# A hybrid decoder step on one core: the attention projections multiply raw x, and the token scale is applied where tiles leave PSUM

## The reference

```python
def rmsnorm(x, g):
    y = xf * lax.rsqrt(jnp.mean(xf * xf, axis=-1, keepdims=True) + EPS)
    return (y * g.astype(jnp.float32)).astype(x.dtype)
...
    h = rmsnorm(x, g)                       # norm_kv
    k, v, fl = jnp.split(h @ w_kv, [D_ATT, 2 * D_ATT], axis=-1)
    logf = jax.nn.log_sigmoid(fl.astype(jnp.float32) + b_f.astype(jnp.float32))
...
    h = rmsnorm(x, g)                       # norm_b
    q, z = jnp.split(h @ w_in, 2, axis=-1)
    o = attend(q.reshape(Bg, T, N_HEADS, HEAD_DIM))
    y = o.reshape(Bg, T, D_ATT) * jax.nn.silu(z)
    return x + y @ w_out
```

## Time and profile before

| | |
|---|---|
| median of 3 runs | 1842.98 us (1842.9 to 1845.61) |
| the profiled execution | 1851.57 us, its span 1850.0 us |
| mean granted TensorE clock | 0.959 of full speed |
| PE busy | 1728.3 us, 93% of the span |
| DVE busy | 848.5 us, 46% |
| ACT busy | 668.2 us, 36% |
| POOL busy | 314.9 us, 17% |

### The profile page before, as it was taken

One profiled execution on the slowest core, in us unless ns is written; L12 is line 12 of the kernel. 1 busy time (PEld: TensorE's weight loads), 2 busy tenths in 40 slices (PEclk: granted clock), 3 DMA queues, 4 the chain that ended last, 5 costly groups with the idle time before them and its releaser, 6 DMA issues.

```text
span 1850.0 us, 31228 instructions
## 1 busy us (share of the span) xinstructions
PE 1728.3 (93%) x10991; PEld 1568.5 (85%) x10991; DVE 848.5 (46%) x1349; ACT 668.2 (36%) x1096; POOL 314.9 (17%) x339
## 2 busy tenths in 40 slices
PE   6999999999999988999999999999866999998997
PEld 5999999999989988888888888888744666668997
DVE  4433333333253366555565556555545333323333
ACT  5211111112043235565655556565534222213322
POOL 4111111100000011222222122222112222210110
PEclk8999999999999989999999999999968999995998
DMA  4111111111201133111101021111225888882002
GB/s 146 36 47 47 47 47 47 47 39 42 75 29 43 29 120 97 37 47 36 58 24 58 24 69 51 43 47 36 86 87 193 306 318 295 330 265 68 29 28 97
DMA packets 173147, 165.08 MB, mean 89 GB/s; under 512 B 19756, under 2 KB 149948, under 8 KB 172966
## 3 DMA queue, kind: packets, MB, share of 16 engines
q1 hardware_dynamic: 162342, 129.51, 22.5%
q0 software_dynamic: 10752, 34.89, 5.2%
HBM read 141.08 MB, written 23.29 MB: 89 GB/s over the span
## 4 chain that ended last, share of the span: by engine, by line
PE 73%; DVE 7%; issue 6%; ACT 5%; DMA 4%; DVEq 2%; ACTq 1%; SPq 1%; POOL 1%; POOLq 0%
PE PS L665 13%; PE PS L667 13%; PE PS L666 13%; PE PS L912 4%; PE PS L853 3%; PE PS L855 3%; PE PS L854 3%; PE PS L964 2%; DMA Vpages<-in_cache_v 2%; DVE small L1677 2%; PE PS L900 2%; DVE pTl L1688 2%; PE PS L883 2%; PE PS L1085 1%; PE PS L884 1%
## 5 line engine op out<-in xcount | busy, mean ns | idle before, releaser
L665 PE MATMUL PS<-Hhi,w_hi 128*128 128x364 f32 (+1 forms) x1320 | 437.4, 331 | 11.4 <-DVE Hlo L1494 6.4
L667 PE MATMUL PS<-Hhi,w_lo 128*128 128x364 f32 (+1 forms) x1320 | 436.8, 331 | 0.0
L666 PE MATMUL PS<-Hlo,w_hi 128*128 128x364 f32 (+1 forms) x1320 | 436.7, 331 | 0.0
L853 PE MATMUL PS<-Hhi,w_hi 128*128 128x364 f32 x744 | 262.2, 352 | 1.1 <-ACT yT L1244 1.1
L665 PEld LDWEIGHTS PS<-Hhi,w_hi 128*128 128x128 f32 x1320 | 251.6, 191 | 12.3 <-issue 8.7
L541 POOL TENSOR_TENSOR w_raw<-w_raw,GT 128x1024 f32<-128x1024 f32 x65 | 127.3, 1960 | 736.3 <-DMA w_raw<-in_w_kv 406.8
L666 PEld LDWEIGHTS PS<-Hlo,w_hi 128*128 128x128 f32 x1320 | 251.6, 191 | 0.0
L667 PEld LDWEIGHTS PS<-Hhi,w_lo 128*128 128x128 f32 x1320 | 251.3, 190 | 0.0
L855 PE MATMUL PS<-Hhi,w_lo 128*128 128x364 f32 x744 | 244.0, 328 | 0.0
L854 PE MATMUL PS<-Hlo,w_hi 128*128 128x364 f32 x744 | 243.9, 328 | 0.0
L1120 ACT ACTIVATE w_hi<-w_raw 128x1024 fp32r<-128x1024 f32 (+1 forms) x97 | 105.5, 1088 | 317.6 <-PE PS L667 295.5
(11 more groups left out here) (285 smaller groups left out, 2585.2 us busy)
## 6 DMA issues: line engine op xcount, KB each, us to landing
Kpages<-in_cache_k SPq DMA_DIRECT2D x64, 512.0 KB, 5.6
Vpages<-in_cache_v POOLq DMA_DIRECT2D x60, 512.0 KB, 6.9
w_raw<-in_w_in_a SPq DMA_DIRECT2D x64, 256.0 KB, 3.0
w_raw<-in_w_ple_gate SPq DMA_DIRECT2D x16, 512.0 KB, 3.8
w_raw<-in_w_kv SPq DMA_DIRECT2D x32, 256.0 KB, 3.2
w_raw<-in_w_in_b SPq DMA_DIRECT2D x32, 256.0 KB, 3.2
parked_x<-X SPq DMA_DIRECT2D x8, 544.0 KB, 6.3
X<-parked_x SPq DMA_DIRECT2D x8, 544.0 KB, 8.4
```

Source lines behind the costliest of these rows:

```text
L665: mm(out, wh, hi[:, k, s:e], start=(k == 0), stop=False)
L666: mm(out, wh, lo[:, k, s:e], start=False, stop=False)
L667: last = mm(out, wl, hi[:, k, s:e], start=False, stop=(k == nk - 1))
L853: mm(out, wh, Hhi[:, k, s:e], start=(k == 0), stop=False)
```

## The change

The chunks are no longer multiplied by the token scale. Hhi and Hlo are made of X itself, partly inside the last tile of feed(0) (chunks 0 to 2) and partly behind it. PE runs the forget tile alone first (u = 0), with norm_sum ahead of its chunk 5 and the spreading of the roots ahead of its chunk 7; then the K tile (u = 1), once the roots have left banks 3 to 5. The scale lies in `rsb`, and every tile that leaves PSUM for the attention layer is multiplied by it: by DVE, in place of ACT's copy. The semaphore act_evac is called evac.

```diff
# tensor
+            def spread_second_roots():
+
                 pe.wait_ge(sems["n1_inv"], 1)
                 for tt in range(9):
                     n = P if tt < 8 else NS
-                    last = tp(PS[:, tt // 4, tt % 4 * P:tt % 4 * P + n], rt[0:n, tt:tt + 1].to_broadcast([n, P]), ident[0:n, 0:n])
+                    last = tp(PS[:, 3 + tt // 4, tt % 4 * P:tt % 4 * P + n], rt[0:n, tt:tt + 1].to_broadcast([n, P]), ident[0:n, 0:n])
...
-            norm_sum()
-
-            pe.wait_ge(sems["w_split"], START["w_split"] + N_B1 + 1)
-            for k in range(KC):
-                pe.wait_ge(sems["h_ready"], 24 + k + 1)
-                for u in range(2):
+            for u in range(2):
+                if u == 1:
+                    pe.wait_ge(sems["w_split"], START["w_split"] + N_B1 + 1)
+                    pe.wait_ge(sems["n1_rs"], 3)
+                for k in range(KC):
+                    if u == 0:
+                        if k == 5:
+                            norm_sum()
+                        if k == 7:
+                            spread_second_roots()
+                        pe.wait_ge(sems["h_ready"], 24 + k + 1)
# scalar, inside and behind feed(0)
+            def raw_hi(k):
+                af(Hhi[:, k, :], X[:, k, :], ACT.Copy).then_inc(sems["h_hi"], 1)
...
+                        if r == 0 and last and u == 1:
+                            for k in range(3):
+                                raw_hi(k)
                         act.wait_ge(sems["x_sum"], START["x_sum"] + 8 * r + 2 * i + u + 1)
                         square(r + 1, 2 * i + u, u)
...
+                    for k in range(3, KC - 2):
+                        raw_hi(k)
+                    act.wait_ge(sems["n1_ps"], 1)
...
+                    for k in range(KC - 2, KC):
+                        raw_hi(k)
+                    w_hi(N_B1 % 2, B_F, gained=34)
...
-            for k in range(KC):
-                act.wait_ge(sems["n1_nx"], k + 1)
-                af(Hhi[:, k, :], sq[1][k % 2], ACT.Copy).then_inc(sems["h_hi"], 1)
...
-            for b, (s, e) in enumerate(BLK):
-                act.wait_ge(sems["block_done"], START["block_done"] + B_B1 + b + 1)
-                af(stK[:, s:e], PS[:, 3 + b, 0:e - s], ACT.Copy).then_inc(sems["act_evac"], 1)
...
-                af((zf, stK, stQ, stQ)[i][:, s:e], PS[:, b, 0:e - s], ACT.Copy,
-                   scale=SCALE if i == 2 else 1.0).then_inc(sems["act_evac"], 1)
# vector
+                        if r == 0 and last and u == 1:
+                            h_lo(X[:, 0, :], 0, 24)
                         ve.drain()
                         add_x(2 * i + u, sg[:, u, :], 0, TT).then_inc(sems["x_sum"], 1)
+                        if r == 0 and last and u == 1:
+                            for k in range(1, 3):
+                                h_lo(X[:, k, :], k, 24)
                         add_square(r + 1, 2 * i + u, u)
...
-            normed(24)
+            for k in range(3, KC - 2):
+                h_lo(X[:, k, :], k, 24)
+            ve.wait_ge(sems["n1_rt"], 2)
+            ve.reciprocal(rt[:, 0:8], rt[:, 0:8])
...
+            for k in range(KC - 2, KC):
+                h_lo(X[:, k, :], k, 24)
+            w_lo(N_B1 % 2, N_B1)
+            ve.wait_ge(sems["n1_wide"], 2)
+            ve.tensor_copy(rsb[:, 512:SEQ], PS[:, 4, :]).then_inc(sems["n1_rs"], 1)
...
+            for b, (s, e) in enumerate(BLK):
+                ve.wait_ge(sems["block_done"], START["block_done"] + B_F + b + 1)
+                tt_(fl[:, s:e], PS[0:H, b, 0:e - s], rsb[0:H, s:e], ALU.mult).then_inc(sems["evac"], 1)
...
+            for b, (s, e) in enumerate(BLK):
+                ve.wait_ge(sems["block_done"], START["block_done"] + B_B1 + b + 1)
+                tt_(stK[:, s:e], PS[:, 3 + b, 0:e - s], rsb[:, s:e], ALU.mult).then_inc(sems["evac"], 1)
...
+            def evacuate(j, i, b):
...
+                ve.wait_ge(sems["block_done"], START["block_done"] + B_B1 + 3 * g_ + b + 1)
+                dst, src = (zf, stK, stQ, stQ)[i][:, s:e], PS[:, b, 0:e - s]
+                if i == 2:
+                    ins = stt(out=dst, in0=src, scalar=SCALE, in1=rsb[:, s:e], op0=ALU.mult, op1=ALU.mult)
+                else:
+                    ins = tt_(dst, src, rsb[:, s:e], ALU.mult)
+                ins.then_inc(sems["evac"], 1)
+                if i and b == NB - 1:
+                    ve.drain().then_inc(sems["staged"], 1)
```

More of the change, by code:

```diff
@@ L745, in norm_sum @@
                     n = P if tt < 8 else NS
-                    last = mm(PS[0:n, 2, NS + tt:NS + tt + 1], ss[:, tt * P:tt * P + n], ones[:, 0:1], start=True, stop=True)
+                    last = mm(PS[0:n, 5, NS + tt:NS + tt + 1], ss[:, tt * P:tt * P + n], ones[:, 0:1], start=True, stop=True)
                 last.then_inc(sems["n1_ps"], 1)
+            def spread_second_roots():
                 pe.wait_ge(sems["n1_inv"], 1)
@@ L848, in dense_piece @@
                 if k == 0:
-                    pe.wait_ge(sems["act_evac"], EA_B1 + (3 * g_ - 3 + b + 1 if not isinstance(j, int) or g_ > 1 else 0))
+                    pe.wait_ge(sems["evac"], EA_B1 + (3 * g_ - 3 + b + 1 if not isinstance(j, int) or g_ > 1 else 0))
                 s, e = BLK[b]
@@ L1217, in feed @@
                 peeled(act, KC // 2, body)
+                if r == 0:
+                    for k in range(3, KC - 2):
+                        raw_hi(k)
+                    act.wait_ge(sems["n1_ps"], 1)
+                    for n, c in ((P, slice(0, 8)), (NS, slice(8, 9))):
+                        af(rt[0:n, c], PS[0:n, 5, NS + c.start:NS + c.stop], ACT.Sqrt, scale=1.0 / D, bias=small[0:n, 31:32]).then_inc(sems["n1_rt"], 1)
+                    for k in range(KC - 2, KC):
+                        raw_hi(k)
+                    w_hi(N_B1 % 2, B_F, gained=34)
+                    act.wait_ge(sems["n1_wide"], 1)
+                    af(rsb[:, 0:512], PS[:, 3, :], ACT.Copy).then_inc(sems["n1_rs"], 1)
+                    act.wait_ge(sems["n1_wide"], 3)
+                    af(rsb[:, SEQ:], PS[:, 5, 0:NS], ACT.Copy).then_inc(sems["n1_rs"], 1)
             out_tiles(N_A2, B_A2)
@@ L1330, in beside @@
                     af(VS[:, :, :, 0:HD], KN[:, 0:8, :].rearrange("p t (h n) -> p t h n", h=2), ACT.Copy).then_inc(sems["v_hi"], 1)
+                if half == 1 and p == 7 and more:
+                    act.wait_ge(sems["evac"], EA_B1 + 3 * (4 * j + 4) + 3)
                 if half == 1 and p in (7, 10) and more:
@@ L1342, in beside @@
                         act.drain().then_inc(sems["kq_hi"], 1)
-                if p in leaves[half] and (more or PIECES * half + p < 24):
-                    evacuate(j, half, *leaves[half][p], attend)
+                if p == 23 and (more or half == 0):
+                    staged_tile(j, 2 * half)
             def half_pair(j, half, more):
@@ L1494, in h_lo @@
                 tt_(Hlo[:, k, :], src, f(Hhi[:, k, :]), ALU.subtract).then_inc(sems["h_ready"], 1)
-            rest = flat[:, 6 * 512:6 * 512 + KEYS]
-            def normed(h0):
-                ve.wait_ge(sems["s_rest"], 1)
-                ve.tensor_copy(RTs[:, 0, 0:KEYS], rest)
-                ve.wait_ge(sems["n1_rt"], 2)
-                ve.reciprocal(rt[:, 0:8], rt[:, 0:8])
-                ve.reciprocal(rt[0:NS, 8:9], rt[0:NS, 8:9])
-                ve.drain().then_inc(sems["n1_inv"], 1)
-                w_lo(N_B1 % 2, N_B1)
-                ve.wait_ge(sems["n1_wide"], 2)
-                ve.tensor_copy(rs[:, 512:SEQ], PS[:, 1, :])
-                ve.wait_ge(sems["n1_rs"], 2)
-                for k in range(KC):
-                    ve.drain()
-                    tt_(sq[1][k % 2], X[:, k, :], rs[:, :], ALU.mult).then_inc(sems["n1_nx"], 1)
-                    if k:
-                        h_lo(sq[1][(k - 1) % 2], k - 1, h0)
-                ve.drain()
-                h_lo(sq[1][1], KC - 1, h0)
             ve.memset(Up[:, 0:2], 0.0)
@@ L1755, in beside @@
                     ve.drain().then_inc(sems["kq_lo"], 1)
+                if p in leaves[half] and (more or PIECES * half + p < 24):
+                    evacuate(j, *leaves[half][p])
                 if half == 0 and attend and p == 25:
```

63 lines of the change are left out of this document (24 added, 39 removed).

## The result

The changed kernel takes 1828.6 us, the median of four runs (1828.01 to 1831.28), against 1843.06 of before in the same comparison: a ratio of 0.991, 95% interval 0.9898 to 0.9923. That is 14 to 19 us less, where 8.7 were forecast (the two medians by themselves differ by 14.5). The profiled execution took 1829.16 us (span 1827.6), 0.6 above its median; the one of before was 8.6 above its own, so the two profiles differ by more than the kernels do. I therefore compare distances inside the traces, and add them up at the end.

What follows compares the result with a forecast made beforehand. PE was taken as the bound in nearly every stage, with the stage before the loop read at DVE's last split. Gains of 5.15 us there and 3.5 in the loop, 8.7 off 1842.98, gave 1834.3 us; range 1828.5 to 1841.

Steps and rivals of the forecast that it cites:

- The loop: Seven pairs of heads: bank copies leave ACT for DVE scalings, gaining 0.5 us a pair, 3.5 us in all.
- the V bank ahead of two pTh: Loop, piece 45: ACT's V copy no longer delays pTh; DVE scales the bank and reaches pTl 0.2 to 0.3 us earlier.
- ceiling of 21.5 us: Loop: PE's waits in seven pairs, 16.3 + 5.2 us, taken as the most any change there can give.
- The clock: Stage before the loop: PE's clock falls again around the sums, costing 3.05 us as before.
- rival 1: Stage: the clock holds because the sums lie between dense stretches; 1831.3 us, chance 0.25.
- PE to the K tile's end: PE from rest's end at 661.97 to the K tile's end: 691.5 at full clock, 694.6 if it falls.
- the wait ahead of chunk 6: Forget tile: PE waits 2.5 us for DVE's low part, slowed by POOL's gain of the next weight tile.
- Behind the K tile: K tile's end to DVE's last split: of 2.0 us saved 1.2 kept, bounds 0 to 2.0.
- the rigid 15.9 us: Last split to DVE's copy of V: SP's transfers in fixed order, 15.9 us, left alone by the change.
- Rival 2: Loop gives nothing, since PE's next wait takes back what one gives; 1837.8 us, chance 0.17.
- Rival 3: Loop: DVE scalings queue ahead of pTl, PE losing 0.53 us each; with three a pair 1848.9 us, chance 0.10.
- Rival 4: Stage does not move, SP's queue or DVE's work past the splits ending last; 1841 us, chance 0.08.

Runs made afterwards that it cites:

- the kernel before with the gain held: Kernel before, POOL's product of the third weight tile with g waits each pair for DVE's first product with silu(z): 1841.83 us, ratio 0.9977.
- K and Q with the gain held: Kernel before, K and Q banks copied by DVE, POOL's third-weight-tile product with g waiting for DVE's first product with silu(z): 1842.78 us, ratio 0.9977.
- the kernel with the sums first: Changed kernel, with norm sums and spreading of the roots moved ahead of the forget tile's chunk 0: 1833.2 us, ratio 0.9935.
- the kernel with doubled sums: Changed kernel, with the 18 one-column sum matmuls made twice ahead of chunk 5: 1836.26 us, ratio 0.9952.
- twelve scalings more a pair: Changed kernel, each scaling made twice; 1841.64 us, ratio 0.9981 with POOL's third-weight-tile product waiting for DVE's first silu(z) product, 1849.83 us, 1.0026 without.

## Why the prediction was off

The direction was right, the sum half of the 17.6 us that the traces show: two terms were mis-sized.

*The loop* failed. "I take 0.5 us a pair" measured 1.23. What the change gives beyond the switch is 82.42 - 82.0 = 0.4 us a pair, near the 0.5: PE's waits for pTl are 1.63 us a pair in the kernel before with the gain held and 1.29 in the changed one. That this comes from the delays that the step named is likely, but not shown. What it missed is 0.85 us from the collision. It had even the cause of it: ACT's 0.46 us ahead of the copy to yT go, and it made of them a pTl that comes about 0.3 us earlier. The product came 0.36 us earlier, and the step did not see that this takes its start past the gain's. Its row stood there: the earlier trace rows show L1697 up to 2139 ns, and the step used it only to settle that a scaling with one SBUF input is not slowed (right: L1735 keeps within 520 to 540 ns in the loop). It did not ask which product took 2139, what POOL did then, who waited behind it, and whether the change moves one of the two. The place that it worked out instead, the V bank ahead of two pTh, is worth 0.05 us a pair by itself. Its ceiling of 21.5 us was too high as well, since 3.3 of the earlier trace rows lie behind the seventh pair.

*The clock* failed. "I take it that the clock falls again" cost 3.05 us in the sum; it stayed at 1.00 in the stage in all ten traces with single sums in the new order. The step took the sums for the cause because the fall stood right behind them. That much it read rightly; the trace of before has

```profile
664.00:664.50 0.50, 0.02 (x1) 0.00 (x0) 0.00 (x0) 0.44 (x3) 0.00 (x0) 0.64 1.04 427
```

so the fall is at 664.14 (0.14 us at 1.00 and 0.36 at 0.50 make the mean of 0.64), 0.1 us behind the sums and ahead of nearly all the idling. But this was one of several places: in the seven traces with the old order the clock fell 0.1 us behind the sums in three (the kernel before; the same with the gain held; K and Q with the gain held) and 2.6 to 3.5 us behind them in four, and it stayed low for 13.7, 10.2 or 6.8 us. And the kernel with the sums first has the same work on PE up to their end, and no fall. So the sums did not settle it, and a forecast from one row took one outcome for the rule. In the kernel with doubled sums the clock fell in the one-column matmuls themselves, with no idling beside them. What decides whether and when it falls stays open. With the clock held, rival 1's mechanism came true; its time, 1831.3, was still too high because of the loop.

*PE to the K tile's end*: 691.5 was worked out with the clock held; it came at 689.83 and the head start was 1.34, so 0.3 less than said. Two errors nearly cancel there: the wait ahead of chunk 6 was 1.15 and not 2.5, and the 144 tile matmuls, with their restarts, took 24.8 us and not 23.9. The step put the contended low part on chunk 6, though by its own numbers that one starts first (673.0, the gain at 673.1); it began at 671.59, before the gain (672.15), and chunk 7's paid.

*Behind the K tile* was right: 1.2 us expected; 18.4 us from the K tile's end to the last split's before, 16.9 now, so 1.5. So was the rigid 15.9 us, and that the stage must be read at the last split.

Rival 2 (the loop gives nothing) is refuted by the pairs. Rival 3 (DVE in the way) did not come, but its danger is real: twelve scalings more a pair cost 1.37 us even with the switch set right, a fifth of their length, so what DVE's 51.6 of 82.0 us leave free is not slack as a share suggests. Most of it is not where the rival put it: with the gain held PE's waits for pTl are 1.72 us a pair instead of 1.29, those for ACT's exponentials (Pb) 1.40 instead of 0.35. Rival 4 (the stage does not move) is refuted; what it feared, SP's queue, bounds the stage's end, only not against this change.

The sum by the measured terms: 8.65 forecast + 3.05 for the clock + 0.8 in the stage + 5.1 in the loop = 17.6 us.

The Trainium skill, SBUF — State Buffer, section Who interferes with whom, has the pair of ports that VectorE and GpSimd share as an exclusive lock: who starts first keeps it for its whole instruction, the other is blocked. The prediction drew on the milder wording of another page and thought of a slowdown. These traces agree with the lock: the product's end follows the gain's by 0.54 or 0.55 us, whether it started 0.36 us behind it, 0.33, 0.04 or in the same hundredth.

What stays open: one more such collision is left in the changed kernel, the low part of K, once a pair (2.23 us in seven of L1710's 14, 1.22 in the others). It stands in the kernel before too; what it is worth wasn't tried. Nor is it settled why executions of one kernel differ by some 8 us with their mean clock (0.957 against 0.965). The traces show where: behind the loop, where the same work takes from 503.0 to 511.2 us over all of them, with the clock low for 94 to 129 us in it.

## What to carry to other kernels

When a line's longest instruction is three times its median, find that instruction, its partner on the other engine and the distance of their starts, before costing anything else: an edit elsewhere can flip who is first, and here a start 0.04 us behind the other instead of 0.03 ahead cost 5.8 us in the trace. If the order matters, write it down as a wait, as one wait alone took 0.2% off the kernel before, rather than leave it to luck. And read what a busy share leaves free by doubling the work: DVE was 63% busy in the loop, and still passed on a fifth of what was added.

## What was not expected of the hardware

One-column matmuls of 2.05 us between dense ones left the granted clock at 1.00, in 4.13 us of them it fell to 0.50 for 3.4 us; with the old order it fell anywhere from 0.1 to 3.5 us behind the same sums. A DVE product of 0.68 us took 2.1 to 2.5 when POOL's gain of 1.92 us had started up to 0.36 us ahead of it or in the same hundredth, and 0.68 when it started 0.02 to 0.05 ahead; POOL's then took 2.43. Moves of banks that gave nothing as V, z, or K and Q gave 1.2 us a pair together, since only together they took the product's start past the gain's.
